# Column groups of TensorE in the products of probabilities and values: two heads on the whole array, and two groups of 64 in place of four of 32

## The reference

```
logits = einsum('bthd,btkhd->bhtk', q, k_sel) * scale + bias      # 256 selected keys a query
p      = softmax(logits)
out    = einsum('bhtk,btkhd->bthd', p, v_sel)                     # (b, t, 8 * 64)
```

## Time and profile before

| | |
|---|---|
| median of 3 runs | 1863.84 us (1859.91 to 1866.31) |
| profiled execution, first to last instruction | 1871.8 us (the time of this execution is not listed apart) |
| mean granted TensorE clock | 0.959 |
| busy in the span | PE 1726.3, PEld 1413.1, DVE 859.4, ACT 653.4, POOL 603.9 us |
| matmul instructions | 11176 |

### The profile page before, as it was taken

The page is one execution under the profiler, slowest core; times in us unless marked ns, Lnnn a source line. Parts: engine busy times, 40 slices in busy tenths (PEclk is TensorE's granted clock), DMA queues, the critical chain, the costliest instruction groups (busy, mean ns, idle before and its releaser), DMA issues.

```text
span 1871.8 us, 28982 instructions
## 1 busy us (share of the span) xinstructions
PE 1726.3 (92%) x11176; PEld 1413.1 (75%) x11176; DVE 859.4 (46%) x1839; ACT 653.4 (35%) x1374; POOL 603.9 (32%) x715
## 2 busy tenths in 40 slices
PE   7888999989967778898789999999999999999998
PEld 6553464789944455565555689999999999999997
DVE  4571889757734444566531343323132323232324
ACT  4464786577232233343321121222222222222123
POOL 1100334266354665555513140404040404040400
PEclk9799999989987899998889999999999999999999
DMA  8301202111184655655571001111110101020202
GB/s 242 93 1 49 92 31 78 49 35 42 43 270 149 177 173 160 175 152 152 149 260 66 0 1 46 46 46 45 39 50 29 60 20 70 10 80 3 98 1 96
DMA packets 68965, 158.03 MB, mean 84 GB/s; under 512 B 9402, under 2 KB 25518, under 8 KB 68608
## 3 DMA queue, kind: packets, MB, share of 16 engines
q1 hardware_dynamic: 47488, 84.91, 13.7%
q0 software_dynamic: 21376, 71.75, 12.8%
HBM read 144.14 MB, written 12.49 MB: 84 GB/s over the span
## 4 chain that ended last, share of the span: by engine, by line
PE 82%; DVE 6%; issue 4%; another core or an unknown queue 3%; ACT 3%; POOL 2%; DMA 1%; SPq 0%; DVEq 0%; ACTq 0%; POOLq 0%
PE psum L1819 7%; PE psum L1817 7%; PE psum L1806 7%; PE psum L1807 7%; PE psum L1805 7%; PE psum L1818 7%; PE psum L1746 6%; PE psum L1360 5%; PE psum L1524 4%; PE psum L1373 3%; PE psum L1549 2%; PE psum L1663 2%; PE psum L1340 2%; PE psum L1641 2%
## 5 line engine op out<-in xcount | busy, mean ns | idle before, releaser
L1805 PE MATMUL psum<-n_hi,wup_hi 128*128 128x384 f32 (+1 forms) x768 | 251.3, 327 | 0.0
L1817 PE MATMUL psum<-h_hi,wdn_hi 128*128 128x384 f32 (+1 forms) x768 | 250.9, 327 | 0.0
L1807 PE MATMUL psum<-n_hi,wup_lo 128*128 128x384 f32 (+1 forms) x768 | 250.8, 327 | 0.0
L1806 PE MATMUL psum<-n_lo,wup_hi 128*128 128x384 f32 (+1 forms) x768 | 250.8, 327 | 0.0
L1819 PE MATMUL psum<-h_hi,wdn_lo 128*128 128x384 f32 (+1 forms) x768 | 250.2, 326 | 0.0
L1818 PE MATMUL psum<-h_lo,wdn_hi 128*128 128x384 f32 (+1 forms) x768 | 250.1, 326 | 0.0
L2441 DVE TENSOR_TENSOR h_lo<-h_full,h_hi 128x384 fp32r<-128x384 f32 (+1 forms) x96 | 112.5, 1184 | 261.5 <-ACT h_hi L1221 252.8
L1213 ACT ACTIVATE hrelu<-psum 128x384 f32<-128x384 f32 (+1 forms) x96 | 45.5, 474 | 502.0 <-PE psum L1807 502.0
L2446 DVE TENSOR_TENSOR x_region<-psum,x_region 128x384 f32<-128x384 f32 (+1 forms) x192 | 102.8, 536 | 252.9 <-PE psum L1819 251.8
L905 POOL TENSOR_TENSOR wup_lo<-wup_full,wup_hi 128x4096 fp32r<-128x4096 f32 x8 | 72.3, 9037 | 421.0 <-ACT wup_hi L1197 421.0
L1075 ACT ACTIVATE arena<-x_region,arena 128x384 bf16<-128x384 f32 (+2 forms) x192 | 166.5, 871 | 23.3 <-POOL arena L851 23.3
(11 more groups left out here) (329 smaller groups left out, 3155.1 us busy)
## 6 DMA issues: line engine op xcount, KB each, us to landing
wup_full<-in_w_up SPq DMA_DIRECT2D x8, 2048.0 KB, 8.0
wdn_full<-in_w_down SPq DMA_DIRECT2D x8, 2048.0 KB, 7.7
arena<-in_x_prompt SPq DMA_DIRECT2D x16, 512.0 KB, 8.8
arena<-in_w_in SPq DMA_DIRECT2D x3, 2048.0 KB, 8.4
arena<-in_w_in SPq DMA_DIRECT2D x12, 512.0 KB, 5.6
out<-arena SPq DMA_DIRECT2D x17, 256.0 KB, 4.5
arena<-in_w_out SPq DMA_DIRECT2D x8, 512.0 KB, 8.4
out<-arena SPq DMA_DIRECT2D x8, 512.0 KB, 2.7
```

Of the source, the lines that this page charges most:

```text
L1805: pe.matmul(b, wu_hi[:, k, col], n_hi[:, k, o:o + w], start=(k == 0), stop=False)
L1806: pe.matmul(b, wu_hi[:, k, col], n_lo[:, k, o:o + w], start=False, stop=False)
L1807: i = pe.matmul(b, wu_lo[:, k, col], n_hi[:, k, o:o + w], start=False, stop=(k == KT - 1))
L1817: pe.matmul(b, wd_hi[:, f, col], h_hi[:, hf, 0:w], start=(f == 0), stop=False)
```

## The change: what it does, and the diff

`values` makes one product a key tile for both heads: 128 value columns stationary, the probabilities of both heads (2 x 128 columns) moving. The result is 128x256 in bank 3; of it the blocks of head 0's columns with head 0's queries and of head 1's with head 1's are used, the other two are not. `pv_done` is counted once a round. `take_values` copies the two blocks in two instructions.

`vals` makes one product a slot: 64 stationary columns (all heads and queries), 512 value columns moving, into partitions 64kk of bank 7 over its whole width. `near_vals` follows suit. The scaling takes the four 32x256 blocks that are the rows' own heads out of the 128x512 result, in four instructions.

```diff
--- before.py
+++ after.py
@@ -779,7 +779,7 @@
             sp.wait_ge(kt_used, NTILE)
             for k in range(5, KT):
                 out_weights(k)
-            sp.wait_ge(pv_done, 2 * NPR)
+            sp.wait_ge(pv_done, NPR)
             for k in range(4):
                 out_weights(k)
             sp.wait_ge(v_used, 4 + 9 * LAST + 1)
@@ -1131,7 +1131,7 @@
 
                 i = q // 4
                 act.wait_ge(pt_ready, PIECES_TO[q] + e * NCHUNK[q] + 1)
-                act.wait_ge(pv_done, 2 * q)
+                act.wait_ge(pv_done, q)
                 k = min(4, i + 1)
                 act.activation(probT[:, e, 0:k, :], bank(2).rearrange("p (a b) -> p a b", a=4)[:, 0:k, :], ACT.Copy).then_inc(pt_act, 1)
 
@@ -1598,14 +1598,12 @@
                     pe.wait_ge(od_ready, b)
                 else:
                     pe.wait_ge(v_back[1], 32)
-                for g in range(4):
-                    pe.matmul(bank(7)[32 * g:32 * g + 32, 0:256], PTw[0:SMP, 32 * g:32 * g + 32],
-                              V[0:SMP, NT - 1, 256 * (g % 2):256 * (g % 2) + 256], start=True, stop=False, skip_group_check=True)
+                for kk in range(2):
+                    pe.matmul(bank(7)[64 * kk:64 * kk + 64, :], PTw[0:SMP, 64 * kk:64 * kk + 64], V[0:SMP, NT - 1, :],
+                              start=True, stop=False, skip_group_check=True)
                 pe.wait_ge(near_in[1], 16 * b + 16)
-                for hh in range(2):
-                    i = pe.matmul(bank(7)[32 * hh:32 * hh + 32, 0:256], PTn[:, 32 * hh:32 * hh + 32], vring[:, r % 4, 0, 256 * hh:256 * hh + 256],
-                                  start=False, stop=False, skip_group_check=True)
-                i.then_inc(v_used, 1)
+                pe.matmul(bank(7)[0:64, :], PTn[:, 0:64], vring[:, r % 4, 0, :], start=False, stop=False,
+                          skip_group_check=True).then_inc(v_used, 1)
 
             def vals(b, x):
 
@@ -1617,10 +1615,9 @@
                 else:
                     ring, r = vring, v_order(b, v_tile(b, x))
                     pe.wait_ge(vring_in[r % 4], in_ring(0, r))
-                for g in range(4):
-                    kk, hh = divmod(g, 2)
-                    i = pe.matmul(bank(7)[32 * g:32 * g + 32, 0:256], PTd[:, n % 2, x % 2 * P + 32 * g:x % 2 * P + 32 * g + 32],
-                                  ring[:, r % 4, kk, 256 * hh:256 * hh + 256],
+                for kk in range(2):
+                    c = x % 2 * P + 64 * kk
+                    i = pe.matmul(bank(7)[64 * kk:64 * kk + 64, :], PTd[:, n % 2, c:c + 64], ring[:, r % 4, kk, :],
                                   start=False, stop=(x == NPAGE_TILES - 1), skip_group_check=True)
                 i.then_inc(v_used, 1)
 
@@ -1675,11 +1672,9 @@
                 if turned_before(4 * (q + 2) + PLAG):
                     pe.wait_ge(pd_done, turned_before(4 * (q + 2) + PLAG))
                 for k in range(i_ + 1):
-                    for e in range(2):
-                        i = pe.matmul(bank(3)[64 * e:64 * e + 64, 0:P], V[:, k, (2 * hp + e) * HD:(2 * hp + e + 1) * HD],
-                                      probT[:, e, k, :], start=(k == 0), stop=(k == i_), skip_group_check=True)
-                        if k == i_:
-                            i.then_inc(pv_done, 1)
+                    i = pe.matmul(bank(3)[:, 0:2 * P], V[:, k, 2 * hp * HD:(2 * hp + 2) * HD], probT[:, :, k, :],
+                                  start=(k == 0), stop=(k == i_), skip_group_check=True)
+                i.then_inc(pv_done, 1)
 
             for u in range(NSUB):
                 b, x = divmod(u, SEQU)
@@ -2310,13 +2305,16 @@
                 if NCHUNK[q] < 2:
                     return
                 dve.wait_ge(pt_ready, PIECES_TO[q] + 2 * e + 2)
-                dve.wait_ge(pv_done, 2 * q)
+                dve.wait_ge(pv_done, q)
                 dve.tensor_copy(probT[:, e, 4:i_ + 1, :], bank(2).rearrange("p (a b) -> p a b", a=4)[:, 0:i_ - 3, :]).then_inc(pt_dve, 1)
 
             def take_values(q):
                 i_, hp = divmod(q, H // 2)
-                dve.wait_ge(pv_done, 2 * q + 2)
-                dve.tensor_copy(mixT[:, hp, i_ * P:(i_ + 1) * P], bank(3)[:, 0:P]).then_inc(val_taken, 1)
+                dve.wait_ge(pv_done, q + 1)
+                for e in range(2):
+                    own = slice(64 * e, 64 * e + 64)
+                    i = dve.tensor_copy(mixT[own, hp, i_ * P:(i_ + 1) * P], bank(3)[own, e * P:(e + 1) * P])
+                i.then_inc(val_taken, 1)
 
             def kt_evac(b, t):
                 m = NPAGE_TILES * b + t
@@ -2363,8 +2361,11 @@
 
                     b = LAST_VALUE[u]
                     dve.wait_ge(v_used, 4 + 9 * (b + 1))
-                    dve.scalar_tensor_tensor(out=od, in0=bank(7)[:, 0:256], scalar=drs[:, b % 2:b % 2 + 1],
-                                             in1=own_head, op0=ALU.mult, op1=ALU.mult).then_inc(od_ready, 1)
+                    for g in range(4):
+                        own, c = slice(32 * g, 32 * g + 32), 256 * (g % 2)
+                        i = dve.scalar_tensor_tensor(out=od[own, :], in0=bank(7)[own, c:c + 256], scalar=drs[own, b % 2:b % 2 + 1],
+                                                     in1=own_head[own, :], op0=ALU.mult, op1=ALU.mult)
+                    i.then_inc(od_ready, 1)
                 if u in LAST_LOGIT:
                     b = LAST_LOGIT[u]
                     dve.wait_ge(l_done, 4 * (b + 1))
```

## The result

| | kernel before | kernel after |
|---|---|---|
| median | 1865.07 us (1859.91 to 1867.35, 4 runs) | 1884.76 us (1884.56 to 1888.15, 4 runs) |
| profiled execution, span | 1871.8 us | 1883.1 us |
| mean granted clock | 0.959 | 0.971 |
| PE busy, instructions | 1726.3 us, 11176 | 1761.4 us, 10584 |

The change costs time: ratio 1.0111 with the interval [1.0087, 1.0135], +20 us. The profiled execution of the kernel after took 1884.92 us, 1.8 more than its span. The two profiled executions lie closer together than the medians: their spans are 11.3 us apart, because the one of the kernel before was slower than all four of its timed runs (span 1871.8 against at most 1867.35). What is read from this pair of traces adds up to 11 us and not to 20.

A forecast was written before the change was run, and what follows sets the result against it. TensorE, busy 92% of the span, though the attention stage is not plainly PE-bound. Of 57 us more PE work 37 lie on the path, 40 with VectorE, less a quarter +30: 1863.84 to 1894 us, range 1862 to 1925.

The forecast's parts named there:

- the likeliest case: Whole kernel: the added work partly reaches the end, time 1878 to 1912 us, chance 0.60.
- Prompt values: Attention stage, 144 key tiles: each costs 0.43 us in place of 0.22, +30.5 us of PE.
- Mode changes: Borders between transposes and prompt values: up to 0.34 us lost per round goes away, taken as -8 us.
- Sample values: Attention stage, 64 page tiles at +0.43 us each and the products ahead of them: together +34.4 us.
- VectorE, +3 us: Split copies and scalings add up to 9.1 + 11.6 us of VectorE, mostly covered: +3 us of 0 to 21.
- The sum: Attention stage: 30.5 - 8 + 34.4 = 57 us more PE work at 2.4 GHz.
- The part on the path: Chain shares 60% and 74% give 37 us, 40 with VectorE; a quarter off for slow stretches and clock: +30 us.
- All of it: Rival: PE is the bound throughout, late ring slots delay every gather: 67 us, 1930 us, chance 0.17.
- Hidden: Rival: gathers pace the attention stage, extra streaming fills PE's 92 idle us; 5 us remain, 1869 us, chance 0.09.
- Faster: Rival: slow stretches and issue cost per instruction; 592 fewer matmuls and mode changes save 25 us: 1839 us, chance 0.14.
- a moving operand in two runs: Value products: might be slower than with a single run; no row shows it, would lie inside "All of it".
- What would show it: Expected trace signs: 0.216 us pitch, tile 1.0 to 1.1 us, PE busy near 405 us, stage 30 us longer, clock 0.90 to 0.93.

The follow-up runs named there:

- prompt_narrow: Kernel before with full-array prompt values, one product a key tile, only one head's 128 probability columns moving, one copy: 1773.4 us, ratio 0.9978.
- before_light: Kernel before with the second slot's gather of each tile left out from the second batch on: 1762.41 us, ratio 0.9923.
- whole change: The complete change measured again against the kernel before: 1884.01 us, ratio 1.0119, on the slower chip; 1827.88 us, ratio 1.0285, on the third chip.
- third chip: The measurement of the third group of runs, where the unchanged kernel before took 1776.72 us.
- dve_only: Kernel before with only VectorE's part: two copies of 64 partitions a round, four scalings of 32 a batch: 1783.53 us, ratio 1.0044.
- light pair: Kernels before and after, both with the second slot's gathers left out from the second batch on: 1762.41 and 1828.31 us.
- slower chip: The measurement of the second group of runs, where the unchanged kernel before took 1866.59 us; in the first measurement it takes as long.
- wide kernels: Two kernels: kernel before, column groups kept, moving columns doubled, with the change's copies or scalings: prompt values 1875.55 us, sample values 1879.31 us.

## Why the prediction came out as it did

Direction and range hold: 1884.8 us against 1894, inside 1862 to 1925, and the likeliest case, the forecast's 1878 to 1912, is the one that came, near its lower end: +20 us where +30 was summed up. Part of that is luck. The case was wide, +14 to +48 us, and its last step was a guess that the runs don't support. Step by step:

- **Prompt values, +30.5 us.** Right. A key tile takes 0.43 us instead of 0.22. In busy time the line grew by 26.2 us; the difference to 30.5 is that the 42.9 us of before were partly spent at the lower clock (0.89 in the stage): where the stage's clock is 0.98 to 0.99, it is 38.4 us (prompt_narrow; 38.5 in before_light) to 68.4 (whole change, third chip), +30.
- **Mode changes, -8 us.** Too large. No run shows what makes PE lose time at the two borders; that it is the step between column groups and the whole array was my estimate. The timeline shows 0.18 us saved at one border and 0.09 at the other, 0.27 x 32 = 8.6 us of PE, but prompt_narrow, which has these savings and no added column, is 3.6 us faster. That kernel still has GpSimd's gathers as the pace for 12.8% of its chain (L865, 515 to 985 us), which would swallow the rest, and waits 0.7 us for output weights at the end; I have not separated this, nor the part of fewer instructions from that of the borders.
- **Sample values, +34.4 us.** Right. A tile takes 0.86 us instead of 0.43 in the timeline. The line grew by 26.9 us here, by 31.6 on the third chip (before_light 43.6, whole change 75.2), against the 27.5 of the step.
- **VectorE, +3 us.** Too low by half. The copies and scalings went by the instruction (288 ns for 64 partitions against 285 for 128, 479 for 32 against 483 for 128): 9 + 11 us more of VectorE, the upper bound that the step had. Alone they cost 6.8 us [4.8 to 10.7 by the interval of the ratio]. My cover, 220 us of free VectorE time, does not help where PE waits for VectorE: the wait of the last `fold` grew from 0.70 to 2.16 us, and that of L1582 for the copies is 8.2 us in before_light and 11.0 in dve_only. The other 2 to 3 us I can't place.
- **The sum.** The 2.4 GHz at which the prediction put it stand in no run; the traces give the clock as a share of full speed, 1.00 and 0.50 in the windows above. 30.5 - 8 + 34.4 + 3 = 60 us; with 3.6 and 6.8 in place of 8 and 3, 68 us. Measured where TensorE leads the chain in both kernels (the light pair): 66 us.
- **The part on the path.** This is the step that failed. From the chain's shares, 60% and 74%, I got 40 us, and then I took "a quarter off" for slow stretches and the clock, 10 us, to reach +30. Neither number describes what was measured. On the third chip the chain's shares were too small a part: 51 of 66 us arrive, and what is lost is some 14 us of slack under GpSimd's gathers. Where the prediction's trace came from, 20 arrive and 46 are lost: in the traces 25 by the clock and 20 to 25 by filled idle time. The sum had 20 us off by the chain's shares and 10 by the guess, 30 in all, for what is 46. The term to size was the idle time of PE, 92 us of the stage, and the share of it at a clock of 0.50, some 22%: about 44 us of PE time were owed to it (353.4 busy against 309.1 where the clock is 0.99, an estimate across two chips), and in the traces the kernel with more PE work gets some 25 of them back.
- **The rivals.** *All of it* (67 us) is what the light pair shows, 66: its mechanism, a late slot that delays each gather, is not even needed, since TensorE is then the pace by itself. *Hidden* is refuted as a whole, though its mechanism has a share: 20 to 25 us of the added work did go into PE's idle time on the slower chip. On the third chip GpSimd's pace does swallow 14 us, which I had excluded by 5.2 against 7.0 us a tile; there the stage of 64 tiles takes 355 us, 5.5 a tile, and the two meet. *Faster* is refuted: with fewer instructions and the old number of columns the gain is 3.6 us and none, not 25, and on the slower chip, where the unnamed waits are, these shrink just as much in the wide kernels, which keep all instructions. That a moving operand in two runs could be slower is answered by the timeline: 256 columns in two runs take 0.215 us, twice the 0.108 of a transpose of 128.
- **What would show it.** The pitch of 0.216, the doubled tile (a tile by itself, x4, 1.08 us), the gap behind the values gone and the one ahead of them halved, GpSimd's longer wait (75.5 us) and a higher clock are all in the trace. The prompt line grew by 26.2 us, not by 28 or more. Stage PE busy was to be near 405 and is 388, the stage is 10 us longer and not 30, and the clock is 0.94, above 0.90 to 0.93: the same failed term again. Of the signs against the forecast, one is half true: PE's idle time fell by 25 us as its busy time grew by 35. Another, slow stretches that shrink with the number of instructions, did not come: they shrank, but as much with all instructions kept.

Shown by runs: that the columns are the price, that instructions and groups are next to nothing of it, VectorE's share, the 14 us under the gathers, and that the added work arrives in full where TensorE leads the chain in both kernels. Only read from traces: that the clock gives back 25 us on the slower chip and filled idle time 20 to 25; no run changed the one without the other. Open: whether the difference between the chips lasts, why the slower one has the unnamed waits at all, and whether the gathers' traffic makes them.

## What to carry to other kernels

Products in different column groups of the array that have the same length ran side by side here. In two groups an instruction of 128 columns added 0.055 us against 0.108 on the whole array, in four groups one of 256 columns 0.054 against 0.215. Merging them into wider ones whose blocks are half thrown away cost the added columns at full price in TensorE's time, 59 to 61 us where the clock was 0.98 to 1.00, and the instructions that went were worth almost nothing: 3.6 us gained for the prompt, 3.4 us lost for the samples. Before an added cost is multiplied by a share of the chain, ask how much of the engine's idle time and of its time at a clock of 0.50 the new work can fill: that part differed between the chips, and on one it was larger than what was left of the cost (46 us against 20). And the same edit should be measured on more than one chip before its size is believed, since here the sign held in all three measurements and the size did not (+20, +17 and +51 us).

## What the runs showed of the hardware that was not expected

- The same kernel before takes 1777 us on two chips and 1865 to 1867 in two other measurements, 5% more, with the runs of a measurement within 0.6% of each other. The difference lies in the attention stage: the last product of `fold` starts at 876 us in dve_only there, which has TensorE's work of the kernel before, and at 961 and 970 us elsewhere (the two traces of the kernel before), and the granted clock of the stage is 0.98 against 0.88 and 0.89. From there to the end of the span it is 902 to 904 us in all three, so the rival that the 88 us lie in the projections or the MLP behind the stage is out.
- The edit's price was +20, +17 and +51 us by the medians of three measurements; the ratios, which come with intervals, are 1.11%, 1.19% and 2.85%.
- These VectorE operations out of PSUM took as long for fewer partitions: a scaling of 32 partitions 479 ns against 483 for 128, a copy of 64 partitions 288 ns against 285 for 128.
- With half of the gathers left out, DMA's share of the stage falls from 0.64 to 0.41 and the time of the kernel after doesn't change (1828.31 against 1827.88 us).
